# Indexer and attention scores from split operands: a 128-row and a 64-row fp32r product in place of a plain f32 one

## What is computed

```python
dots = jnp.einsum("bthd,bsd->bths", iq_b, ik)                 # index scores
score = jnp.einsum("bth,bths->bts", iw_b, jax.nn.relu(dots))
score = jnp.where(causal[None], score, -jnp.inf)
_, idx = lax.top_k(score, k_top)                              # 128 keys of each query
k_sel, v_sel = gather(k, idx), gather(v, idx)
logits = jnp.einsum("bthd,btkd->bhtk", q_b, k_sel) * (HEAD_DIM ** -0.5)   # dsa scores
logits = logits + bias                                        # by bucketed distance
p = jax.nn.softmax(jnp.where(valid, logits, -jnp.inf))
o = jnp.einsum("bhtk,btkd->bthd", p, v_sel)
```

## Time and profile before

| | |
|---|---|
| median of 3 runs | 1060.88 us (1060.54 to 1061.25) |
| profiled execution: span, first to last instruction | 1059.3 us |
| what the median has beside that span | 1.6 us |
| TensorE busy | 1049.7 us, 99% |
| VectorE, ScalarE, GpSimd busy | 509.0, 448.8, 400.2 us |
| index scores, line 2169 | from 396.5 to 419.7 us |
| dsa scores, line 1940 | from 516 to 570.5 us |

### The profile page before, as it was taken

One profiled execution on the slowest core, in us unless ns is written; L12 is line 12 of the kernel. 1 busy time (PEld: TensorE's weight loads), 2 busy tenths in 40 slices (PEclk: granted clock), 3 DMA queues, 4 the chain that ended last, 5 costly groups with the idle time before them and its releaser, 6 DMA issues.

```text
span 1059.3 us, 14455 instructions
## 1 busy us (share of the span) xinstructions
PE 1049.7 (99%) x5545; PEld 844.1 (80%) x5545; DVE 509.0 (48%) x1061; ACT 448.8 (42%) x788; POOL 400.2 (38%) x300
## 2 busy tenths in 40 slices
PE   9999999999999999999999999999999999999997
PEld 8877897767678876888777888888888888888886
DVE  6766788875752316998587344230000000032444
ACT  6444457676653425233465414342221221233533
POOL 3455520001025333446000255434435354465772
PEclk9999999999999999999999999999999999999999
DMA  9541141201032331332221232223232323323221
GB/s 298 184 120 51 34 119 41 75 17 44 28 120 80 72 117 43 101 99 80 80 80 41 80 104 95 91 77 110 80 118 79 114 84 104 114 80 100 82 97 80
DMA packets 84724, 95.72 MB, mean 90 GB/s; under 512 B 8121, under 2 KB 70930, under 8 KB 84666
## 3 DMA queue, kind: packets, MB, share of 16 engines
q1 hardware_dynamic: 83706, 92.46, 28.0%
q0 software_dynamic: 560, 2.12, 0.6%
q10 hardware_dynamic: 400, 0.35, 0.1%
HBM read 92.80 MB, written 2.12 MB: 90 GB/s over the span
## 4 chain that ended last, share of the span: by engine, by line
PE 94%; DVE 4%; ACT 1%; issue 1%; POOL 0%; DVEq 0%; ACTq 0%; POOLq 0%
PE bank L1882 56%; PE bank L2194 23%; PE bank L1940 4%; PE bank L1971 3%; PE bank L2012 3%; PE bank L1988 1%; DVE L L1478 1%; PE bank L2169 1%; PE bank L1833 1%; PE bank L2098 1%; PE bank L2045 1%; DVE L L1524 1%; DVE pool L1483 0%; PE bank L2001 0%; PE bank L1964 0%
## 5 line engine op out<-in xcount | busy, mean ns | idle before, releaser
L1042 POOL TENSOR_TENSOR w_lo<-raw,w_hi 128x512 fp32r<-128x512 f32 (+1 forms) x190 | 267.2, 1436 | 415.7 <-ACT w_hi L1104 403.0
L1882 PE MATMUL bank<-h_hi,w_hi 128*128 128x512 f32 (+1 forms) x560 | 224.0, 400 | 0.3 <-ACT h_hi L1315 0.2
L1882 PE MATMUL bank<-h_hi,w_lo 128*128 128x512 f32 (+1 forms) x560 | 218.6, 390 | 0.0
L1882 PE MATMUL bank<-h_lo,w_hi 128*128 128x512 f32 (+1 forms) x560 | 217.8, 390 | 0.0
L1082 POOL TENSOR_TENSOR w_lo<-raw,w_hi 128x512 fp32r<-128x512 f32 x88 | 110.7, 1290 | 133.5 <-ACT w_hi L1353 67.1
L1104 ACT ACTIVATE w_hi<-raw 128x512 fp32r<-128x512 f32 (+3 forms) x94 | 111.2, 1213 | 116.1 <-PE bank L1882 113.8
L1882 PE MATMUL bank<-w_hi,h_hi 128*128 128x512 f32 (+2 forms) x397 | 145.3, 366 | 0.0
L1882 PE MATMUL bank<-w_lo,h_hi 128*128 128x512 f32 (+2 forms) x397 | 144.5, 364 | 0.0
L1882 PE MATMUL bank<-w_hi,h_lo 128*128 128x512 f32 (+2 forms) x397 | 144.5, 364 | 0.0
L2194 PE MATMUL bank<-h_hi,w_hi 128*128 128x512 f32 x352 | 137.1, 389 | 0.0
L2194 PE MATMUL bank<-h_hi,w_lo 128*128 128x512 f32 x352 | 137.0, 389 | 0.0
(11 more groups left out here) (213 smaller groups left out, 1260.3 us busy)
## 6 DMA issues: line engine op xcount, KB each, us to landing
raw<-in_w_in SPq DMA_DIRECT2D x29, 1024.0 KB, 5.3
raw<-in_w_ffn_gate SPq DMA_DIRECT2D x11, 1024.0 KB, 5.4
raw<-in_w_ffn_up SPq DMA_DIRECT2D x11, 1024.0 KB, 5.4
raw<-in_w_out SPq DMA_DIRECT2D x8, 1024.0 KB, 5.0
raw<-in_w_ffn_down SPq DMA_DIRECT2D x8, 1024.0 KB, 5.1
raw<-in_w_in SPq DMA_DIRECT2D x8, 512.0 KB, 4.6
pool<-in_cmp_w SPq DMA_DIRECT2D x4, 1024.0 KB, 9.1
raw<-in_w_ffn_down SPq DMA_DIRECT2D x4, 768.0 KB, 4.3
```

The costliest lines, as they stand in the source:

```text
L1042: nc.gpsimd.tensor_tensor(w_lo[:, u.n % 2, cols], raw[:, u.n % 2, cols], w_hi[:, u.n % 2, cols].bitcast(F32), ALU.subtract).then_inc(lo_do ...
L1882: ins = mm(bank[t.bank][0:t.m, 0:u.width if u.token else T], stationary, moving, start=first and n == 0, stop=last and n == len(products) ...
```

## The change

Both operands of the scores are split into a high fp32r part and the rest. For each head a stack of 128 rows holds the high half of the query in one 64-row half and its rest in the other (`iq_s0`, `iq_s1`, `q2_s0`, `q2_s1`: head 0 has its high part in rows 0 to 63, head 1 in rows 64 to 127). The high part of the key stands in both halves (`ik2_hi`, `k2_hi`), and so does its rest (`ik2_lo`, `k2_lo`). A score is then one full-array product, stack times high key (hi*hi + lo*hi in one pass over 128 rows), and one of 64 rows, the stack's high half times the key's rest, added to it in the same bank. The two 64-row products of the two heads are issued side by side, behind the two 128-row ones.

The split adds evacuations: ScalarE writes the high halves (two copies of 64 rows instead of one of 128), VectorE the rests (two operations a tile, four more for `kik`), and a bank of an iq or q2 tile is free when VectorE is done. The new arrays need 12 KB more per partition; the scratch memory of software DMA is set to 4096 bytes, where the kernel before leaves it at its default.

```diff
-        elif t.kind in ("cmp", "kik", "z", "nz"):
+        elif t.kind in ("cmp", "kik", "z", "nz", "iq", "q2"):
             t.norms, t.auxes = count["norm_done"], count["aux_done"]
-            t.sc = upto("sc_evac") if t.kind in ("z", "nz") else None
+            t.sc = upto("sc_evac") if t.kind in ("z", "nz", "iq", "q2") else None
             t.ve = upto("ve_evac")
             left[t.bank] = [("ve_evac", t.ve)]
...
+        def split_operands(job, c, g, i):
+            rows = slice(DH * c, DH * c + DH)
+            toks = slice(P * i, P * i + P)
+            n = P * (i + 1)
+            stack = (q2_s0, q2_s1)[c]
+            return (stack[:, g, toks], k2_hi[:, 0:n]), (stack[rows, g, toks], k2_lo[rows, 0:n])
...
                 if kind == "iq":
-                    act_fn(iq[:, idx, :], src, ACT.Copy).then_inc(sc_evac, 1)
+                    act_fn(iq_s0[0:DH, idx, :], src[0:DH, :], ACT.Copy)
+                    act_fn(iq_s1[DH:P, idx, :], src[DH:P, :], ACT.Copy).then_inc(sc_evac, 1)
                 if kind == "q2":
-                    act_fn(q2[:, idx, :], src, ACT.Copy, scale=-(DH ** -0.5)).then_inc(sc_evac, 1)
+                    act_fn(q2_s0[0:DH, idx, :], src[0:DH, :], ACT.Copy, scale=-(DH ** -0.5))
+                    act_fn(q2_s1[DH:P, idx, :], src[DH:P, :], ACT.Copy, scale=-(DH ** -0.5)).then_inc(sc_evac, 1)
...
                     for r in range(2):
-                        v.tensor_copy(k2[DH * r:DH * r + DH, :], src[0:DH, :])
-                        ins = v.tensor_copy(ik2[DH * r:DH * r + DH, :], src[DH:P, :])
+                        v.tensor_copy(k2_hi[DH * r:DH * r + DH, :], src[0:DH, :])
+                        ins = v.tensor_copy(ik2_hi[DH * r:DH * r + DH, :], src[DH:P, :])
+                    chain(ins)
+                    for r in range(2):
+                        v.tensor_tensor(k2_lo[DH * r:DH * r + DH, :], src[0:DH, :], k2_hi[0:DH, :].bitcast(F32),
+                                        ALU.subtract)
+                        ins = v.tensor_tensor(ik2_lo[DH * r:DH * r + DH, :], src[DH:P, :], ik2_hi[DH:P, :].bitcast(F32),
+                                              ALU.subtract)
                     ins.then_inc(ve_evac, 1)
+                if kind == "iq":
+                    ve.wait_ge(sc_evac, t.sc)
+                    v.tensor_tensor(iq_s0[DH:P, idx, :], src[0:DH, :], iq_s0[0:DH, idx, :].bitcast(F32), ALU.subtract)
+                    v.tensor_tensor(iq_s1[0:DH, idx, :], src[DH:P, :], iq_s1[DH:P, idx, :].bitcast(F32), ALU.subtract)\
+                        .then_inc(ve_evac, 1)
...
                 for p, (g, i) in enumerate(job.parts):
+                    last = p == len(job.parts) - 1
+                    if job.which == "dsa":
+                        pairs = [split_operands(job, c, g, i) for c in range(2)]
+                        for c in range(2):
+                            mm(bank[S_BANKS[c]][:, columns(job, p)], *pairs[c][0], start=True, stop=False)
+                        for c in range(2):
+                            ins = mm(bank[S_BANKS[c]][:, columns(job, p)], *pairs[c][1], start=False, stop=True)
+                            if last:
+                                ins.then_inc(s_done, 1)
+                        continue
...
                 if which == "dsa" and k == 0:
                     pe.wait_ge(ix_relu, 3 * DSA_HEADS)
-                    pe.wait_ge(sc_evac, q_u[1].tiles[-1].sc)
-                    pe.wait_ge(ve_evac, kik_u.tiles[0].ve)
+                    pe.wait_ge(ve_evac, q_u[1].tiles[-1].ve)
...
                     i, w = 1 + e["m"] // 4, P * (2 + e["m"] // 4)
+                    if e["m"] >= 2:
+                        pe.wait_ge(ix_relu, 2 * e["m"] - 2)
+                    toks = slice(P * i, P * i + P)
                     for half in range(2):
-                        r = 2 * e["m"] + half
+                        mm(bank[4 + (2 * e["m"] + half) % 4][:, 0:w], (iq_s0, iq_s1)[half][:, e["m"] % 4, toks],
+                           ik2_hi[:, 0:w], start=True, stop=False)
+                    for half in range(2):
                         rows = slice(DH * half, DH * half + DH)
-                        if r >= 4:
-                            pe.wait_ge(ix_relu, r - 3 + (1 - half))
-                        mm(bank[4 + r % 4][:, 0:w], iq[rows, e["m"] % 4, P * i:P * i + P], ik2[rows, 0:w],
-                           start=True, stop=True).then_inc(ix_s, 1)
+                        mm(bank[4 + (2 * e["m"] + half) % 4][:, 0:w], (iq_s0, iq_s1)[half][rows, e["m"] % 4, toks],
+                           ik2_lo[rows, 0:w], start=False, stop=True).then_inc(ix_s, 1)
...
-    nc = bacc.Bacc("TRN2", target_bir_lowering=False, num_devices=1)
+    nc = bacc.Bacc("TRN2", target_bir_lowering=False, num_devices=1, dynamic_dma_scratch_size=4096)
```

More of the change, by code:

```diff
@@ L720, in build @@
         xres = sb("xres", [P, NT, D])
-        zs = sb("zs", [P, NT, D])
-        pool = sb("pool", [P, 16384])
+        with nc.sbuf_tensor("zs", [P, NT, D], F32) as zs, nc.sbuf_tensor("pool", [P, 16384], F32) as pool:
+            pass
+        ik2_hi = sb("ik2_hi", [P, T], F32R)
+        above_ik2 = sb("above_ik2", [P, NT * D - T])
+        q2_s0 = sb("q2_s0", [P, 4, T], F32R)
+        k2_hi = sb("k2_hi", [P, T], F32R)
+        above_k2 = sb("above_k2", [P, 11 * T])
+        iq_s0 = sb("iq_s0", [P, 4, T], F32R)
+        iq_s1 = sb("iq_s1", [P, 4, T], F32R)
+        above_iq = sb("above_iq", [P, 8 * T])
+        q2_s1 = sb("q2_s1", [P, 4, T], F32R)
+        k2_lo = sb("k2_lo", [P, T], F32R)
+        ik2_lo = sb("ik2_lo", [P, T], F32R)
         with nc.sbuf_tensor("L", [P, LRING, T], F32) as L, nc.sbuf_tensor("PT", [P, PRING, T], F32) as PT:
@@ L773, in build @@
         hidden_rows = region(13824, P)
-        q2, k2, v2 = region(0, 4, T), region(2048, T), region(2560, NT, DH)
+        v2 = region(2560, NT, DH)
         pm = region(2816, 1280)
         bh = region(4096, DSA_HEADS, T)
-        iq = region(8192, 4, T)
         cc, cx = region(12288, 4, T), region(14336, 4, T)
@@ L781, in build @@
         ya = zflat[:, 2048:4096].rearrange("p (m n) -> p m n", m=4)
-        ik2, work = zflat[:, 0:512], zflat[:, 512:1664]
+        work = zflat[:, 512:1664]
         iw = zflat[:, 1664:1664 + 8 * NT].rearrange("p (i h) -> p i h", i=NT)
@@ L946, in operands @@
                 return dq[rows, g, toks], dk[rows, g, 0:n]
-            if job.which == "nsa":
-                return nq[rows, g, toks], kd[rows, 2 * job.br + (g // 2 != c), 0:n]
-            return q2[rows, g, toks], k2[rows, 0:n]
+            return nq[rows, g, toks], kd[rows, 2 * job.br + (g // 2 != c), 0:n]
+        def split_operands(job, c, g, i):
[4 more added lines that the diff above has]
+            return (stack[:, g, toks], k2_hi[:, 0:n]), (stack[rows, g, toks], k2_lo[rows, 0:n])
         block = ctx.enter_context(nc.Block())
@@ L1459, in evacuate @@
                     for r in range(2):
-                        v.tensor_copy(k2[DH * r:DH * r + DH, :], src[0:DH, :])
-                        ins = v.tensor_copy(ik2[DH * r:DH * r + DH, :], src[DH:P, :])
-                    ins.then_inc(ve_evac, 1)
+                        v.tensor_copy(k2_hi[DH * r:DH * r + DH, :], src[0:DH, :])
[6 more added lines that the diff above has]
+                                              ALU.subtract)
+                    ins.then_inc(ve_evac, 1)
+                if kind == "iq":
[3 more added lines that the diff above has]
+                        .then_inc(ve_evac, 1)
+                if kind == "q2":
+                    ve.wait_ge(sc_evac, t.sc)
+                    v.scalar_tensor_tensor(q2_s0[DH:P, idx, :], src[0:DH, :], -(DH ** -0.5),
+                                           q2_s0[0:DH, idx, :].bitcast(F32), ALU.mult, ALU.subtract)
+                    v.scalar_tensor_tensor(q2_s1[0:DH, idx, :], src[DH:P, :], -(DH ** -0.5),
+                                           q2_s1[DH:P, idx, :].bitcast(F32), ALU.mult, ALU.subtract).then_inc(ve_evac, 1)
                 if kind == "branch_a":
@@ L1940, in score @@
                         ins = mm(bank[S_BANKS[c]][:, columns(job, p)], q, k, start=True, stop=True)
-                        if p == len(job.parts) - 1:
+                        if last:
                             ins.then_inc(s_done, 1)
@@ L2158, in _ @@
                 if kind == "index_starts":
-                    pe.wait_ge(sc_evac, iq_u[1].tiles[-1].sc)
                     pe.wait_ge(ve_evac, kik_u.tiles[0].ve)
```

## The result

The changed kernel takes 1062.99 us (median of 15 runs, 1062.71 to 1063.36); the kernel before took 1060.88 us (15 runs, 1060.54 to 1061.4) beside it. The ratio is 1.002, 95% interval 1.0013 to 1.0027: 2.1 us slower, at the border of what the prediction called measurable, inside its range and 0.6 us under its time.

The account below looks back on a forecast made before the run. TensorE's queue was taken to bound the kernel: less streaming but twelve added round trips (4.9 us) summed to +2.0 to +3.5, taken +2.7, on 1060.88, giving 1063.6 us; range 1060.7 to 1065.4.

Parts of the forecast that it names:

- The bound: TensorE's queue, busy every microsecond in 396 to 420 and 516 to 592 us; time added there moves the end one for one.
- The price of a round trip: On TensorE, going from 128-row products to 64-row ones and back costs 0.41 us whatever the columns; twelve added trips, 4.9 us.
- The terms without 128 columns: Score work on TensorE: job of 512 -0.18 us, 256+256 +0.25, index pieces +0.25, +0.14 and +0.03 at 256, 384, 512.
- The term of 128+384: Four two-part dsa jobs on TensorE: +0.35 to +0.71 us each, together +1.4 to +2.8, middle +2.1.
- the lower bound: 128+384 jobs with 128-column products 0.11 us apart and the pair's streaming at 0.053: +0.35 a job, sum +2.0.
- the plain rate of 0.213: Upper bound for 128-column products in the 128+384 jobs: four passes, 0.213 us for a product and for the pair.
- The work moved off TensorE: Added ScalarE copies (4.8 us) and VectorE operations (13.6 us), later bank release and smaller scratch: costed at nothing.
- A hidden load on entry: Rival: 64-row fp32r loads run behind the preceding 128-row product, 28 entries lose 0.10 us each: -2.8, 1060.8 us; chance 0.14.
- That a product begins before its load is complete: Skill statement weighed for the rival of hidden loads; said not to show at row-count changes, so given little weight.
- Halves in turn: Rival: the fp32r halves of a pair don't run side by side, streaming 4.05 us more: +6.8, 1067.6 us; chance 0.08.
- Another queue: Rival: GpSimd held by the smaller scratch (+1.6 us) or a relu late by VectorE's tile work (+1.4 to 2): 1065.2; chance 0.12.
- its chances for these two: For the whole kernel's time: slower 0.62, same 0.32, with the boundary to slower at 1063.0 us.

Follow-up runs that it names:

- grouping: Changed kernel with all 128-row products of a job or index piece issued before all its 64-row pairs: 1058.33 us; with each bank's sum opened only once, 1058.41 us.
- the kernel with the evacuations alone: Kernel before, scores untouched, plus the change's added ScalarE and VectorE operations written to spare arrays, later bank release and smaller scratch: 1061.04 us.
- a second pair of 512 columns: Changed kernel with each pair of 64-row products issued twice in a row: 1067.6 us.
- the kernel whose index pieces are over 1 us shorter: Changed kernel with the 64-row products left out, so the scores lack the term with the key's rest: 1051.01 us.
- full rows: Changed kernel with the second product taking all 128 rows of the stack against the key's rest, no 64-row product left in the scores: 1057.83 us.

## Why the prediction came out as it did

**The bound** was right: every microsecond was added in TensorE's queue in the two stretches, none outside.

**The price of a round trip**, 0.41 us and independent of the columns, was right: 0.38 to 0.41 for each trip that grouping saves where no 128-column product stands, and nothing left in the index pieces of 256 columns without one. The Trainium skill (TensorEngine Tiling (Array Packing), "Key Properties") says that a change of the tiling mode, other than one of the tile, drains TensorE. The trace agrees in so far as every change to 64 rows and back costs time, and gives the price that the page doesn't; whether the array runs empty no record here shows.

**The terms without 128 columns** were right: a job of 512 -0.17 (predicted -0.18), of 256+256 +0.24 (+0.25), the index pieces +0.23, +0.15 and +0.06 (+0.25, +0.14, +0.03).

**The term of 128+384 was mis-sized.** The prediction took the middle of two bounds, +0.53 a job; measured are +0.28 to +0.30, less than even the lower bound's +0.35. The step that failed is the choice between them: a 128-column product was put halfway from 0.11 to the plain rate of 0.213. In the rows after, the two of them and the way in take 0.27 (515.96 to 516.23) where the lower bound has 2x0.11+0.09 = 0.31 and the upper 0.52; the second of the two starts 0.057 behind the first, and 128 columns at 2.4 GHz are 0.053. That second product by itself, and its load:

```profile
516.02 0.28 PE L1977 MATMUL bank<-k_hi,q_s 128*128 128x128 f32 x1
```

```profile
515.97 0.19 PEld L1977 LDWEIGHTS bank<-k_hi,q_s 128*128 128x128 f32 x1
```

The pair behind them takes 0.26 to the next start, against 0.32, 0.37 and 0.43 at 256, 384 and 512 columns: steps of 0.05 to 0.06, the one-pass rate. So the rate followed the number format, as the rows at 256 columns had shown, and the plain rate of four passes had no say. Four jobs at 0.23 to 0.25 less make 1.0 us and more than explain the 0.8 by which the sum was too high (+2.7 taken, +1.9 in the queue); some hundredths in the other terms go the other way. The sum with the lower bound was +2.0.

**The work moved off TensorE** costs the queue nothing, as priced; the kernel with the evacuations alone shows it.

**The rivals.** A hidden load on entry fell: in each of the 56 changes of row count of the two stretches the load starts within 0.01 us of its product. That a product begins before its load is complete, which the prediction held not to show at these changes, isn't what decides: by the records it does, there as in the streams (a load's is 0.19 long), but at a change no load runs ahead. Halves in turn fell: they start together, and a second pair of 512 columns adds 0.23. Another queue fell for this change, and came up only in the kernel whose index pieces are over 1 us shorter. The measured 1062.99 us are a loss clear of the noise (ratio 1.0013 to 1.0027), but they stand at the boundary of 1063.0 that the prediction had drawn between slower and no change, so its chances for these two are neither borne out nor refuted.

**The median** is 0.2 us more over before than the queue shows, and this part lies outside the span. Over all runs the time has 1.82 us (median) beside the span of the same execution in the kernel before, 2.06 in the changed one, and 1.97 to 2.06 in every kernel of the experiments. The one with the evacuations alone is among them: its span is that of the kernel before (both 1059.0 us), its median 0.14 us over. So this part comes with the added evacuations, their arrays or the smaller scratch, and not with the scores; which of these it is was not tested. The 1.6 us given ahead of the prediction came from a median and the span of a slower execution.

## What to carry to other kernels

Count changes of tile shape, not only columns: here a pair of fewer rows between full ones costs 0.41 us beside its streaming, nearly two streamed products of 512 columns, and filling the other rows with a needless term was cheaper for the whole kernel than leaving the shape. It was not cheaper everywhere: an index piece of 256 columns costs 0.96 with full rows and 1.10 grouped, but a job of 128+384 with the values and transposes behind it 3.19 with full rows and 3.11 grouped. No run took the cheaper form at each place. When both kinds are needed, issue all of one kind and then all of the other. When a price is unknown at a new size, take the rate from rows of the same number format at other sizes rather than from rows of the same size in another format; what goes by the load rather than by the rate can still be read from the latter, as the 0.11 us between products of 128 columns that came back in the full-row kernel.

## What the hardware showed beside

- Products behind a 128-column fp32r product start at two distances: 0.057 us (two of them behind a 512-column product, in the jobs of 128+384), or 0.11 (every further one there in the full-row kernel, and the first of 384 columns in the grouped one, 0.113). The 81 ns that the prediction cited from the Trainium skill (TensorE: Matmul & The Clock Gate, "Back-to-back issue gap") lie between the two, and no run here shows them. The loads tell the two apart: the first product's load started with the 512-column product ahead (515.74), the second's not before the first product itself (515.97), and its product 0.05 behind that. From there on, in the full-row kernel, loads start 0.11 apart and each product 0.05 to 0.06 behind its own.
- VectorE's accumulations, which read `L` and `zs`, became slower while GpSimd subtracted. In the changed kernel, one of them, and the operation of GpSimd beside it:

```profile
402.08 1.33 DVE L1831 SCALAR_TENSOR_TENSOR zs<-L,zs 128x256 f32<-128x256 f32 x1
```

```profile
401.65 1.47 POOL L1058 TENSOR_TENSOR w_lo<-raw,w_hi 128x512 fp32r<-128x512 f32 x1
```

  GpSimd subtracts from 400.42 to 405.98. The four accumulations of 256 columns that start in this time take 1.32 to 1.45 us, the other three 0.48 to 0.49; those of 512 columns take 1.59 to 1.77 beside GpSimd and 0.75 without. Each of these eight slow ones ends 0.28 us (256 columns) or 0.55 us (512) behind the end of one of GpSimd's operations, here 403.41 behind 403.13, and the kernel before shows the same. So VectorE seems to be held until GpSimd's operation is over; no run took GpSimd's work away.
